# Issuing the expert-row gathers of a PEER layer in pairs of one table instead of in turn

## The chip, the cores and the metric

The kernel runs on one core of one Trainium2 chip. The metric is the device time of one execution in microseconds; the median of several runs counts. The engines are TensorE (PE in the profile), VectorE (DVE), ScalarE (ACT), GpSimd (POOL, here called Pool) and SyncE (SP). Indirect transfers, which fetch one table row per partition, are issued by Pool.

## What is computed

One decoder layer on 1024 tokens of width 1024, all in float32: attention and a convolution side by side, an output projection, and then the expert retrieval (PEER), in which nearly all the bytes are moved. Cut to its core:

```python
for each chunk of 128 tokens:
    s1, s2 = scores of the query halves against 128 + 128 keys, for 8 heads
    top_s, experts = best 16 of the 16 x 16 candidate sums          # 128 experts per token
    gates = softmax(top_s)
    act = gelu(einsum('chkd,cd->chk', u_tab[experts], xc))           # one u row per expert
    y = einsum('chk,chkd->cd', gates * act, v_tab[experts])          # one v row per expert
```

Each of the two tables has 16384 rows of 4 KB. Each token reads its own 128 rows from each of them.

## The kernel before, in words

There are two phases. Phase 0 projects all tokens and brings the first chunk up to its list of experts. Phase 1 runs over the 8 chunks; in step (c, f) it retrieves the rows of chunk c while it computes the attention, convolution, mixing, query and search of chunk f = c + 1 ("the front") in between. A step has 128 slots, one for each expert. The program is written out by hand for each engine, and each engine executes its list in order; semaphores connect them.

In slot s:

- Pool (`step` and `gather` at the gpsimd block) issues the gather of u row s of chunk c, and of v row s - 20 (LAG = 20; in the first 20 slots these are the last v rows of the chunk before). A gather brings 128 rows of 4 KB, one to each partition, 512 KB.
- VectorE (`dot_row`, L1744) multiplies the landed u row by the tokens' vector and sums; this increments `dotted` and frees the u slot. Then come the pieces of the front that VectorE has in this slot.
- ScalarE applies gelu to 16 dots at a time and builds for each expert a diagonal matrix of its weights (`spread_weight`, L1577).
- TensorE (`add_row`, L1433) multiplies the diagonal by the landed v row and adds it to the sum y in PSUM: two products of 512 columns, each shown in the records as two MATMULs, so four for one row; this increments `row_added` and frees the v slot. Then come TensorE's pieces of the front in that slot.
- In slot 20, `begin_y` (L1422) starts the sum of the new chunk, once ScalarE has copied the old one out (L1583).

Rows land in two rings of six slots, `ring_u` and `ring_v`. Before each gather Pool waits until the row that had the slot six rows earlier was used:

```python
if before >= 0 and kind == "u":
    hold(pool, dotted, before + 1, pool_passed)
...
elif before >= 0:
    hold(pool, row_added, pe_rows(before), pool_passed)
```

Since Pool works in order, a gather that has to wait holds back all gathers behind it. After the last chunk's slots, `tail` issues the last 20 v rows. VectorE adds five of the last 20 aside (`SIDE`), TensorE the others.

Of the kernel before, what the change touches and what calls it, by code (L numbers as in the profile page):

```python
# [37 lines left out]
ROWS = PH * TOPK  # L38
# [4 lines left out]
LAG = 20  # L43
SLOTS = ROWS
# [40 lines left out]
def row_of(c, e):  # L85

    return ROWS * c + e


def hold(eng, sem, value, passed):  # L90

    eng.wait_ge(sem, value)
    eng.sem_inc(passed, 1)


def later(i):

    return not isinstance(i, int) or i > 0
# [1111 lines left out]
def phase1(nc, S, base, psum, ident, ident_b, mask, kT, vals, keys_bd, w_kept, wo_sb, actT, qT,  # L1210
# [38 lines left out]
    def pe_rows(n):  # L1249

        return n + 1 - len([t for t in SIDE if row_of(CHUNKS - 1, t) <= n])
# [23 lines left out]
    def over_chunks(step):  # L1275

        step(None, 0)
        for f in range(1, CHUNKS):
            step(f - 1, f)
        step(CHUNKS - 1, None)  # L1280

    with nc.Block() as block:

        @block.sync
        def _(sp):
            def load_front(f):
                if later(f):
                    sp.wait_ge(S.z_ready, UNITS * f)
                    sp.dma_start(qT[:, :, :].rearrange("p b t -> p (b t)"),
                                 qT_spill[f]).then_inc(S.q_in, 16)  # L1290
                    sp.wait_ge(S.tapped, TAP_OPS * f)
                    sp.dma_start(conv_in[:, :, :], hT_spill[:, :, f * P:f * P + HALO + P]).then_inc(S.c_in, 16)
                    sp.wait_ge(y_begun, f)
                    sp.dma_start(S.h_res[:, :], x[0, f * P:(f + 1) * P, :]).then_inc(S.x_in, 16)

            def store(c):
                sp.wait_ge(y_copied, c + 1)
                sp.dma_start(out[0, c * P:(c + 1) * P, :], y_out[:, :]).then_inc(y_stored, 16)

            def step(c, f):  # L1300
                if f is not None:
                    load_front(f)
                if c is not None and later(c):
                    store(c - 1)

            over_chunks(step)
            store(CHUNKS - 1)
            sp.wait_ge(y_stored, 16 * CHUNKS)

        @block.gpsimd  # L1310
        def _(pool):
            def step(c, f):
                if c is None:
                    return
                hold(pool, S.experts_done, c + 1, pool_passed)
                for s in range(SLOTS):
                    gather("u", c, s)
                    if s >= LAG:
                        gather("v", c, s - LAG)
                    elif later(c):  # L1320
                        gather("v", c - 1, s - LAG + ROWS)

            def gather(kind, c, e):

                n = row_of(c, e)
                before = n - RING[kind]
                if before >= 0 and kind == "u":
                    hold(pool, dotted, before + 1, pool_passed)
                elif before >= 0 and in_side(before // ROWS, before % ROWS):
                    hold(pool, side_added, SIDE.index(before % ROWS) + 1, pool_passed)  # L1330
                elif before >= 0:
                    hold(pool, row_added, pe_rows(before), pool_passed)
                at = n % RING[kind]
                nc.gpsimd.indirect_dma_start(  # L1334
                    ring[kind][:, at, :], None, peer_u[0] if kind == "u" else peer_v[0],
                    bass.IndirectOffsetOnAxis(S.experts[c % 2][:, e:e + 1], 0)).then_inc(row_in[kind][at], 16)

            def tail():
                for e in range(ROWS - LAG, ROWS):
                    gather("v", CHUNKS - 1, e)  # L1340

            over_chunks(step)
            tail()

# [535 lines left out]
```

## Time and profile before

| | |
|---|---|
| median of 3 runs | 3085.05 us (3084.18 to 3085.98) |
| profiled execution | 3088.14 us, span 3086.4 us |
| TensorE / VectorE / ScalarE / Pool busy | 87% / 70% / 29% / 64% of the span |
| gathers | 2048, of 0.524 MB each |
| first gather, last gather issued | 365 us, 3074 us |
| data rate over the span | 363 GB/s |

A busy TensorE is not one at its peak, as the ends of its matmuls are modelled. In a timeline a line gives the start, the duration, the engine with the line of the source, what was done, and in brackets how long the engine sat idle before it and what ended that. Several instructions of one kind that follow on each other are merged, with their number. The name behind the arrow is inferred from semaphore events and can be that of another event close in time; for a wait on `row_added` or `dotted` the order of the program tells which it is.

### The profile page before, as it was taken

The numbers are of one execution on the slowest core, as the hardware profiler recorded it, in microseconds if no ns is written. First come the engines' busy times: TensorE is split into PE (matmuls) and PEld (weight loads), VectorE is DVE, ScalarE is ACT, GpSimd is POOL, SyncE is SP. The second block draws the span as 40 slices with busy tenths as digits, with TensorE's granted clock in tenths as the row PEclk, the third lists the DMA queues.
The fourth block names the chain that finished last, engine by engine and source line by source line (L and its number), as shares of the span: only waits on it lengthen the run. The fifth ranks groups of instructions, "written<-read, shape, count | busy, mean of one in ns | idle before, by whom it ended". The sixth has DMA issues, their size and how long they took to land.

```text
span 3086.4 us, 30095 instructions
## 1 busy us (share of the span) xinstructions
PE 2677.0 (87%) x7609; PEld 1207.5 (39%) x7609; DVE 2156.1 (70%) x5205; ACT 879.9 (29%) x2053; POOL 1986.3 (64%) x2062
## 2 busy tenths in 40 slices
PE   8999669878997889889997999799988999777777
PEld 4455324423352335334442445234433445222222
DVE  1161997886789667977788778977787767844443
ACT  2233123124221342135212542146213641111111
POOL 1000167777777777777777776776777677777775
PEclk9999879999999999999999999999999999999999
DMA  6011399999999999999999999999999999999998
GB/s 241 29 33 72 129 340 409 409 406 410 408 396 400 409 408 408 400 407 409 405 388 410 409 408 403 405 407 383 409 409 409 371 401 409 409 410 410 410 409 338
DMA packets 320463, 1121.47 MB, mean 363 GB/s; under 512 B 36465, under 2 KB 44681, under 8 KB 320296
## 3 DMA queue, kind: packets, MB, share of 16 engines
q0 software_dynamic: 294912, 1073.87, 88.0%
q1 hardware_dynamic: 25384, 45.72, 4.2%
q8 instruction: 62, 1.02, 0.1%
q14 instruction: 105, 0.86, 0.1%
HBM read 1111.01 MB, written 8.45 MB: 363 GB/s over the span
## 4 chain that ended last, share of the span: by engine, by line
PE 33%; DMA 24%; issue 12%; POOL 9%; DVE 8%; ACT 2%; POOLq 0%; ACTq 0%; DVEq 0%; SPq 0%
PE psum L1433 23%; DMA ring_v<-in_peer_v,experts 19%; POOL ring_v L1334 5%; DMA ring_u<-in_peer_u,experts 5%; POOL ring_u L1334 4%; PE psum L949 3%; DVE ring_u L1744 3%; PE psum L970 3%; PE psum L1365 1%; PE psum L1391 1%; ACT diag L1577 1%; PE psum L1381 1%; DVE acc L1700 1%; DVE top_i L1081 1%; DVE relu_z L1084 1%
## 5 line engine op out<-in xcount | busy, mean ns | idle before, releaser
L1433 PE MATMUL psum<-ring_v,diag 128*128 128x512 f32 x4076 | 1949.8, 604 | 331.3 <-DMA ring_v<-in_peer_v,experts 200.3
L1744 DVE CUSTOM_DVE_ANT_0 ring_u<-ring_u,psum 128x1024 f32<-128x1024 f32 x1024 | 1240.9, 1217 | 545.9 <-DMA ring_u<-in_peer_u,experts 540.3
L1334 POOL DMA_INDIRECT ring_u<-in_peer_u,experts x1024 | 983.7, 961 | 692.4 <-issue 594.2
L1334 POOL DMA_INDIRECT ring_v<-in_peer_v,experts x1024 | 991.8, 969 | 395.9 <-issue 243.4
L1433 PEld LDWEIGHTS psum<-ring_v,diag 128*128 128x128 f32 x4076 | 710.5, 190 | 1336.6 <-issue 961.3
L1577 ACT ACTIVATE diag<-ident,weights 128x128 f32<-128x128 f32 x1019 | 364.4, 393 | 771.1 <-PE psum L1433 550.6
L483 PE MATMUL psum<-w_sb,xnT 128*128 128x512 f32 x560 | 246.9, 599 | 0.3 <-DMA w_sb<-in_w_in 0.3
L1700 DVE SCALAR_TENSOR_TENSOR acc<-conv_in,taps,acc 128x128 f32<-128x128 f32 x840 | 239.6, 347 | 0.1
L483 PEld LDWEIGHTS psum<-w_sb,xnT 128*128 128x128 f32 x560 | 106.4, 193 | 128.1 <-issue 124.0
L970 PEld LDWEIGHTS psum<-actT,w_kept 128*128 128x128 f32 x1024 | 129.9, 192 | 47.4 <-issue 47.4
L1669 DVE TENSOR_TENSOR_SCAN log_keep<-log_keep,relu_z 128x256 f32<-128x256 f32 (+3 forms) x88 | 90.3, 1027 | 59.5 <-ACT log_keep L1510 58.1
L970 PE MATMUL psum<-actT,w_kept 128*128 128x128 f32 x1024 | 130.3, 275 | 0.0
L1525 ACT ACTIVATE attT<-psum 128x256 f32<-128x256 f32 (+3 forms) x88 | 44.9, 510 | 243.3 <-PE psum L1381 243.3
L949 PE MATMUL psum<-wo_sb,actT 128*128 128x512 f32 x224 | 112.1, 592 | 0.0
L1568 ACT ACTIVATE geld<-dots 128x16 f32<-128x16 f32 x64 | 13.8, 216 | 341.8 <-DVE dots L1744 341.5
L1365 PE MATMUL psum<-kT,qT 64*128 64x512 f32 (+3 forms) x176 | 86.6, 573 | 7.9 <-DMA qT<-qT_spill 6.9
L1744 DVE DVE_READ_ACCUMULATOR2_ANT dots<- 128x1 f32 x1024 | 85.0, 83 | 0.0
L1391 PEld LDWEIGHTS psum<-vals,attT 128*128 128x128 f32 x560 | 72.9, 195 | 29.2 <-issue 25.9
L1516 ACT ACTIVATE relu_z<-relu_z 128x256 f32<-128x256 f32 (+3 forms) x88 | 47.2, 536 | 117.7 <-DVE relu_z L1671 117.7
L1381 PE MATMUL psum<-ident,relu_z 128*128 128x128 f32 x280 | 48.2, 285 | 33.3 <-ACT relu_z L1516 33.2
L1391 PE MATMUL psum<-vals,attT 128*128 128x64 f32 x560 | 71.3, 275 | 2.5 <-ACT attT L1525 2.3
L790 DVE TENSOR_REDUCE qk_stat<-squares 128x16 f32<-128x1024 f32 x8 | 9.8, 1220 | 85.1 <-ACT squares L640 85.1
(188 smaller groups left out, 1556.3 us busy)
## 6 DMA issues: line engine op xcount, KB each, us to landing
ring_u<-in_peer_u,experts POOLq DMA_INDIRECT x1024, 10.0
ring_v<-in_peer_v,experts POOLq DMA_INDIRECT x1024, 9.9
w_sb<-in_w_in SPq DMA_DIRECT2D x4, 2048.0 KB, 19.6
x_in<-in_x SPq DMA_DIRECT2D x8, 512.0 KB, 4.0
w_kept<-in_w_out SPq DMA_DIRECT2D x1, 4096.0 KB, 13.6
h_res<-in_x SPq DMA_DIRECT2D x8, 512.0 KB, 6.7
w_kept<-in_peer_wq SPq DMA_DIRECT2D x1, 4096.0 KB, 14.5
wo_sb<-in_w_out SPq DMA_DIRECT2D x1, 4096.0 KB, 12.5
```

The costliest lines, as they stand in the source:

```text
L483: last = nc.tensor.matmul(ps[g], xT(i)[:, k, :], w_sb[:, g, k, :], start=k == 0, stop=k == KT_D - 1)
L949: product = nc.tensor.matmul(z[0][:, j * BANK:(j + 1) * BANK], S.actT[:, k, :], wo_sb[:, k, j * BANK:(j + 1) * BANK], start=k == 0, stop=k ...
L970: product = nc.tensor.matmul(z[0][:, h * P:(h + 1) * P], wq_sb[:, k, h * P:(h + 1) * P], S.actT[:, k, :], start=k == 0, stop=k == KT_D - 1)
L1334: nc.gpsimd.indirect_dma_start(ring[kind][:, at, :], None, peer_u[0] if kind == "u" else peer_v[0], bass.IndirectOffsetOnAxis(S.experts[c ...
L1365: last = nc.tensor.matmul(z, qT[lo:lo + HD, a // 2, :], kT[lo:lo + HD, a // 2, lo_key:hi_key], start=True, stop=not has_own)
L1381: last = nc.tensor.transpose(t_ps[:, s - lo:s - lo + P], S.relu_z[a % 2][:, s:s + P], ident[:, :])
L1391: last = nc.tensor.matmul(o_ps[:, a * HD:(a + 1) * HD], S.attT[:, b, :], vals[:, b, a * HD:(a + 1) * HD], start=n == 0, stop=n == len(orde ...
L1433: last = nc.tensor.matmul(y_ps[:, j * BANK:(j + 1) * BANK], diag[:, e % DIAGS, :], ring["v"][:, n % RING["v"], j * BANK:(j + 1) * BANK], s ...
L1577: nc.scalar.activation(diag[:, e % DIAGS, :], ident[:, :], ACT.Copy, scale=weights[:, e:e + 1]).then_inc(diagonal, 1)
L1669: nc.vector.tensor_tensor_scan(l[:, back], l[:, back], r[:, back], carry, ALU.add, ALU.add).then_inc(S.summed, counts(f))
L1700: nc.vector.scalar_tensor_tensor(out=acc[:, c, :], in0=conv_in[:, c, t:t + P], scalar=taps[:, c, t:t + 1], in1=acc[:, c, :], op0=ALU.mult, ...
L1744: nc.vector.tensor_tensor_reduce(out=row, in0=row, in1=hn, scale=1.0, scalar=0.0, op0=ALU.mult, op1=ALU.add, accum_out=dots[:, e:e + 1]).t ...
```

## The change

Pool's loop goes over two slots at a time. It issues the two u gathers of the two slots and then their two v gathers. Which slot, semaphore and value each gather waits for, and which list of experts it reads, are as before; the other engines' programs are the same.

```diff
                 hold(pool, S.experts_done, c + 1, pool_passed)
-                for s in range(SLOTS):
+                for s in range(0, SLOTS, 2):
                     gather("u", c, s)
-                    if s >= LAG:
-                        gather("v", c, s - LAG)
-                    elif later(c):
-                        gather("v", c - 1, s - LAG + ROWS)
+                    gather("u", c, s + 1)
+                    for n in (s, s + 1):
+                        if n >= LAG:
+                            gather("v", c, n - LAG)
+                        elif later(c):
+                            gather("v", c - 1, n - LAG + ROWS)
```

First Pool's queue where phase 1 begins. `experts0` is the list of experts of the even chunks; "x5" says that a row stands five times in a row. Before:

```order
L1334 DMA ring_u_1823<-in_peer_u,experts0_73 128x1024 [waits experts_done]
L1334 DMA ring_u_1823<-in_peer_u,experts0_73 128x1024 x5
L1334 DMA ring_u_1823<-in_peer_u,experts0_73 128x1024 [waits dotted] x15
L1334 DMA ring_v_1824<-in_peer_v,experts0_73 128x1024
L1334 DMA ring_u_1823<-in_peer_u,experts0_73 128x1024 [waits dotted]
L1334 DMA ring_v_1824<-in_peer_v,experts0_73 128x1024
```

The same place in the changed kernel:

```order
L1336 DMA ring_u_1823<-in_peer_u,experts0_73 128x1024 [waits experts_done]
L1336 DMA ring_u_1823<-in_peer_u,experts0_73 128x1024 x5
L1336 DMA ring_u_1823<-in_peer_u,experts0_73 128x1024 [waits dotted] x16
L1336 DMA ring_v_1824<-in_peer_v,experts0_73 128x1024 x2
L1336 DMA ring_u_1823<-in_peer_u,experts0_73 128x1024 [waits dotted] x2
```

22 u gathers stand ahead of the first v gather instead of 21, and from there on they go two by two.

Then Pool's queue where the second chunk begins (`experts1` is its list, `experts0` still that of the first chunk's last v rows). Before:

```order
L1334 DMA ring_v_1824<-in_peer_v,experts0_73 128x1024 [waits row_added]
L1334 DMA ring_u_1823<-in_peer_u,experts1_74 128x1024 [waits experts_done,dotted]
L1334 DMA ring_v_1824<-in_peer_v,experts0_73 128x1024 [waits row_added]
L1334 DMA ring_u_1823<-in_peer_u,experts1_74 128x1024 [waits dotted]
L1334 DMA ring_v_1824<-in_peer_v,experts0_73 128x1024 [waits row_added]
```

And in the changed kernel:

```order
L1336 DMA ring_v_1824<-in_peer_v,experts0_73 128x1024 [waits row_added] x2
L1336 DMA ring_u_1823<-in_peer_u,experts1_74 128x1024 [waits experts_done,dotted]
L1336 DMA ring_u_1823<-in_peer_u,experts1_74 128x1024 [waits dotted]
L1336 DMA ring_v_1824<-in_peer_v,experts0_73 128x1024 [waits row_added] x2
L1336 DMA ring_u_1823<-in_peer_u,experts1_74 128x1024 [waits dotted] x2
```

The second u gather of a pair has moved ahead of the first v gather, with its wait for `dotted`; the waits themselves are the same. An even chunk length and an even LAG keep the pairs aligned with the slots throughout.

## Rows read from the trace of the kernel before

**Rows 1.** The page: busy time by engine, and the data rate in 40 slices.

```profile
PE 2677.0 (87%) x7609; PEld 1207.5 (39%) x7609; DVE 2156.1 (70%) x5205; ACT 879.9 (29%) x2053; POOL 1986.3 (64%) x2062
...
GB/s 241 29 33 72 129 340 409 409 406 410 408 396 400 409 408 408 400 407 409 405 388 410 409 408 403 405 407 383 409 409 409 371 401 409 409 410 410 410 409 338
```

**Rows 2.** The page's DMA queues: packets, MB, share of 16 engines.

```profile
q0 software_dynamic: 294912, 1073.87, 88.0%
```

**Rows 3.** Windows: length, busy PE, PEld, DVE, ACT, POOL; PEclk, DMA share, GB/s.

```profile
410.00:3040.00 2630.00, 2283.83 (x6430) 1010.74 (x6430) 1960.93 (x4636) 760.71 (x1810) 1935.68 (x2008) 1.00 1.02 404
400.00:450.00 50.00, 31.98 (x81) 14.20 (x82) 46.75 (x119) 18.62 (x46) 34.97 (x38) 0.80 0.95 356
900.00:950.00 50.00, 42.59 (x117) 18.94 (x117) 48.94 (x188) 7.05 (x20) 35.96 (x37) 1.00 0.99 376
2100.00:2150.00 50.00, 47.98 (x172) 24.84 (x172) 35.97 (x68) 28.04 (x61) 32.57 (x35) 0.97 0.98 371
2440.00:2450.00 10.00, 8.58 (x16) 3.86 (x17) 3.52 (x7) 2.99 (x6) 3.70 (x4) 0.66 0.97 345
2450.00:2500.00 50.00, 49.32 (x188) 26.19 (x187) 39.48 (x72) 31.79 (x67) 37.78 (x37) 1.00 0.97 365
2700.00:2750.00 50.00, 38.54 (x80) 13.48 (x80) 25.02 (x41) 7.29 (x20) 37.66 (x41) 1.00 1.03 409
```

**Rows 4.** Groups of lines, Pool, 410 to 3040 us: busy, mean ns, idle before.

```profile
L1334 POOL DMA_INDIRECT ring_v<-in_peer_v,experts x1004 | 972.2, 968 | 379.5 <-issue 240.7 <-DVE dots L1744 75.2 <-PE psum L1433 63.6
L1334 POOL DMA_INDIRECT ring_u<-in_peer_u,experts x1004 | 964.0, 960 | 314.5 <-issue 238.2 <-PE psum L1433 49.1 <-DVE dots L1744 27.2
```

**Rows 5.** Timeline of all engines near 1510 us, while the front mixes.

```profile
1508.67 1.88 PE L1433 MATMUL psum<-ring_v,diag 128*128 128x512 f32 x4
...
1510.38 1.02 PE L949 MATMUL psum<-wo_sb,actT 128*128 128x512 f32 x2
...
1511.24 1.88 PE L1433 MATMUL psum<-ring_v,diag 128*128 128x512 f32 x4
1511.33 1.22 DVE L1744 CUSTOM_DVE_ANT_0 ring_u<-ring_u,psum 128x1024 f32<-128x1024 f32 x1 [1.29 <-DMA ring_u<-in_peer_u,experts]
...
1512.47 0.08 DVE L1744 DVE_READ_ACCUMULATOR2_ANT dots<- 128x1 f32 x1
...
1512.60 1.03 POOL L1334 DMA_INDIRECT ring_u<-in_peer_u,experts  x1 [0.30 <-issue]
...
1513.94 0.93 POOL L1334 DMA_INDIRECT ring_v<-in_peer_v,experts  x1 [0.30 <-issue]
```

**Rows 6.** ring_v, issue to landing: issued 1500 to 1520, then 940 to 950.

```profile
DMA to landing us min/median/max: 11.4/11.5/12.4
...
DMA to landing us min/median/max: 7.2/7.3/7.4
```

**Rows 7.** Waits of TensorE, 420 to 3040 us: total, times, longest.

```profile
PE psum L1433 <- DMA ring_v<-in_peer_v,experts: 195.3, 304, 1.6
```

**Rows 8.** Timeline where the chunk's sum begins, all engines.

```profile
2440.26 1.02 ACT L1583 ACTIVATE hn_next<-psum 128x1024 f32<-128x1024 f32 x1
...
2441.42 3.75 PE L1422 MATMUL psum<-h_res,ident 128*128 128x512 f32 x4 [1.75 <-ACT hn_next L1583]
...
2442.45 0.93 POOL L1334 DMA_INDIRECT ring_u<-in_peer_u,experts  x1 [0.30 <-DVE dots L1744]
...
2444.97 3.14 PE L1433 MATMUL psum<-ring_v,diag 128*128 128x512 f32 x4
...
2448.91 0.93 POOL L1334 DMA_INDIRECT ring_v<-in_peer_v,experts  x1 [5.54 <-PE psum L1433]
...
2450.15 0.93 POOL L1334 DMA_INDIRECT ring_u<-in_peer_u,experts  x1 [0.30 <-issue]
...
2451.36 1.28 DVE L1669 TENSOR_TENSOR_SCAN log_keep<-log_keep,relu_z 128x512 f32<-128x512 f32 x1 [7.85 <-ACT log_keep L1510]
```

**Rows 9.** Timeline of TensorE in a stretch with rows only.

```profile
2720.44 1.96 PE L1433 MATMUL psum<-ring_v,diag 128*128 128x512 f32 x4 [0.61 <-DMA ring_v<-in_peer_v,experts]
```

## The prediction

> **What bounds the kernel now.** I read the page's slices first. From the seventh slice on the GB/s row stands near 409, slice after slice, while no engine is that steadily full [rows 1]. The software queue moved 1073.87 MB, which is 2048 gathers of 0.524 MB [rows 2]; at 409 GB/s one gather takes 0.524/409 = 1.28 us, a u and v pair 2.56 us. The steady part is therefore paced by the transfers.
>
> Then the question is how often the transfers are not fed. Over 410 to 3040 us the mean is 404 GB/s against 409.5 when full [rows 3], so (409.5 - 404)/409.5 x 2630 = 35 us are lost there; 6.5 us of these ((409.5 - 356)/409.5 x 50) belong to the start between 400 and 450 us, where only u rows come. The remaining 29 us sit in a few dips: 900 to 950 us (376 GB/s, 4.1 us), 2100 to 2150 (371, 4.7 us), 2440 to 2450 (345, 1.6 us), 2450 to 2500 (365, 5.4 us) [rows 3], and smaller ones. Of the page's slices 7 to 39, eight stand below 405 (396, 400, 400, 388, 403, 383, 371, 401) [rows 1]. A new order of the same 2048 gathers can win at most these 29 us; the floor of 1.28 us each stays.
>
> Third, who holds Pool. Its gathers cost 960 ns (u) and 968 ns (v), and the smallest gap before one is 0.30 us (the u gather in [rows 5]). 1004 such gaps are 301 us. Before the u gathers the idle time is 314.5 us, 13 us more than that; before the v gathers it is 379.5 us, 78 us more [rows 4]. So Pool waits nearly always for a v slot, which TensorE frees, and hardly ever for a u slot, which VectorE frees. Pool has 0.94 + 0.30 = 1.24 us per gather against the transfers' 1.28: once its queue is drained it gains only 0.04 us per gather.
>
> **How full the queue is.** Where it is full, the cycle of a v slot shows why. At 1511.24 us a row starts on TensorE, ends 1.88 us later at 1513.12, and the v gather that waited for it starts at 1513.94, 0.82 us after [rows 5]. Issue to landing is 11.5 us there [rows 6]. 11.5 + 1.88 + 0.82 = 14.2 of the 12 x 1.28 = 15.4 us between two uses of a slot; 1.2 us go into the wait before the row. Around 940 us issue to landing is 7.3 us [rows 6] and the dip of 900 to 950 us is open: I take 7.3 as an estimate of the drained end. The cushion is 11.5 - 7.3 = about 4 us.
>
> **The change, part by part.** No gather, wait or byte is added or removed on any engine. In each group of four, the first u and the last v keep their places. The odd u comes one place (1.28 us) earlier; the even v comes one place later. A slot's previous user is still 12 places ahead, since rings of 6 are three pairs.
>
> *Pool's own time*: same 1.24 us per gather, four in 4.96 us against 5.12 us of transfer. Zero, covered by the transfers; without that cover it would be zero too, the count being the same.
>
> *The odd u, earlier*: VectorE needs 1.22 + 0.08 = 1.30 us per dot [rows 5], so two that land 1.28 us apart are taken in turn. Work between them delays the odd dot and holds the odd u's successor, and the two v gathers queued behind it on Pool. The u slots had 13 us of waiting in the whole run against 78 for v [rows 4], so I take zero; the bound above is in the slower rival.
>
> *The even v, later*: here is a cost. TensorE is in order. Where it has mixing work between rows (two matmuls, 0.86 us from 1510.38 to 1511.24, after 1.71 us of row from 1508.67), rows come 2.57 us apart [rows 5]. Two v rows landing 1.28 us apart leave the second waiting 2.57 - 1.28 = 1.29 us longer than an evenly spaced one. Its slot frees later, so the full queue is 11.5 - 1.3 = 10.2 us deep. In a stretch with rows only, the row takes 1.72 us, and the loss is 1.72 - 1.28 = 0.44 us. While the cushion holds this costs nothing. A dip that begins with a full cushion then loses up to 1.29 us more; one that begins with the queue already drained loses nothing more, since Pool runs free. If TensorE is behind anyway, rows wait for it and not for landings, and the price is zero. Of the waits of rows, 304 (195.3 us) end on a landed v row [rows 7], of about 1000, so TensorE is often not behind. I count four dips of the first kind (the search stages of four chunks, of which 900 us is one) at the middle of 0 and 1.29: 4 x 0.65 = +2.6 us; bounds 0 and +5.2.
>
> *The odd u ahead of a blocked v*: here is a gain. At the chunk's 20th slot TensorE waits for the copy of the finished sum, then starts a new one. At 2442.45 us Pool issues a u and is then held 5.54 us, until 2448.91, for the first row of the new chunk; that held gather is v 6, an even one. The next u starts at 2450.15, after the minimal 0.30 us, and VectorE had finished no dot since about 2443.5 (it sat idle for 7.85 us before 2451.36) [rows 8]. Its slot was thus free all along. In the new order this u is issued before the hold, one transfer, 1.28 us, more for the queue in a place where the rate fell to 345 [rows 3]. Two chunks (2100, 2440) have such a dip: bounds 0 and -2.56, I take half, -1.3 us. The other half is given back because VectorE, stalled on the attention chain, holds the following odd u.
>
> *Start and end*: the first v goes out one u later (1.24 us), inside the start that VectorE limits; at the end the last v has its old place, and the chain of odd rows that leads to it too. I take +0.6, bounds 0 and +1.28.
>
> Sum: 2.6 - 1.3 + 0.6 = +1.9 us. The profiled execution took 3088.14 us (its span is 3086.4), so it would take 3090.0; the median of the runs, 3.1 us below the profiled one, moves from 3085.05 to **3087.0 us**. That is +0.06%: a measurement of this kernel can't tell anything within 0.2% (6.2 us) from no change.
>
> **Rivals.**
> *Cushion lost everywhere (slower).* The 1.29 us is lost at each of the eight slow slices [rows 1], and at the two deep dips twice, as the odd u's hold adds the same: 10 x 1.29 = +13 us, 3098. For it: Pool gains 0.04 us per gather, so a lost cushion of 1.29 us needs 32 gathers to return. Against it: at 7.3 us the queue was already drained in the middle of dips, and there order can't matter. It decides from five full losses on (6.4 us).
> *TensorE's clock (slower).* At 2441.42 TensorE starts after 1.75 us idle; the granted clock over 2440 to 2450 us is 0.66, a mix of the levels 2.4 and 1.2 GHz, and a row takes 3.14 us against 1.88 [rows 3, 5, 8]. Now, with rows only, TensorE idles 0.61 us before each row [rows 9]; with pairs it would idle 5.12 - 1.72 - 1.96 = 1.44 us before every second one. If the clock falls there, a row takes 1.26 us more. This decides only once more than (2.56 - 1.88)/1.26 = 54% of rows are slow; before that rows still keep pace. Were 80% slow over the 133 pitches of 2700 to 3040 us, it would cost 133 x (0.8 x 3.14 + 0.2 x 1.88 - 2.56) = 44 us. The Trainium skill (TensorE: Matmul & The Clock Gate, Part 1: The HAM clock gate) says that idleness lowers TensorE's clock and sustained activity restores it; by that, slow rows that fill the gaps should bring the clock back. The trace agrees in that the next window has 1.00 [rows 3]. So I give it little.
> *Holds covered (faster).* If the earlier u covers v holds wherever the rate dips and TensorE is behind at all of them, the cost term is zero and each of the eight slices gains up to 1.28 us: -10 us, 3075. For it: v is what holds Pool. Against it: the odd v is not issued sooner, so at the end of each group of four nothing is ahead. It decides from five full gains on.
> *The order on chip does nothing*: covered by my forecast.
>
> **How the numbers follow.** Forecast (a sum within 6.2 us of zero) 0.52; cushion lost everywhere 0.25; clock 0.05; holds covered 0.18. So slower 0.30, same 0.52, faster 0.18. The likeliest alone is 3083 to 3091 us (its bounds: -2.6 to +6.5 us). For 8 in 10 I reach into both sides, to 3077 and 3099.
>
> **What would show it.** Right: the GB/s row stays at 409 between dips, the number of gathers and Pool's time per gather are unchanged, issue to landing near 1500 us drops from 11.5 to about 10.2 us, waits of TensorE on v rows become fewer and longer, the hold at the new chunk's first row shrinks by about 1.2 us, and 2450 to 2500 us moves little. Wrong: a deeper queue, Pool waiting for u slots (much more than 13 us), clock below 1.00 in the row-only stretches, or a steady rate other than 409, which would mean that the order of tables itself matters to the transfers; no row of before bears on that.

## The result: slower, by more than forecast

| | before | after |
|---|---|---|
| median of 6 runs each | 3084.61 us (3083.91 to 3087.91) | 3101.54 us (3096.12 to 3103.47) |
| ratio after/before | | 1.0049, 95% interval 1.0038 to 1.006 |
| profiled execution | 3088.14 us | 3096.74 us, span 3094.9 us |

The change costs 16.9 us at the median (15.3 us at the mean, from which the ratio is taken); +1.9 us were forecast. The two profiled executions lie 8.6 us apart: that of before is above its median, that of after near the lowest of its runs. What the two traces show can therefore account for 8.6 us, not for all 16.9.

The page of after, busy time and rate, answers to [rows 1]:

```profile
PE 2630.9 (85%) x7609; PEld 1233.1 (40%) x7609; DVE 2139.8 (69%) x5205; ACT 882.0 (28%) x2053; POOL 2010.3 (65%) x2062
...
GB/s 240 29 32 72 133 338 409 396 400 409 408 404 390 404 408 409 399 400 407 408 383 399 409 408 396 407 400 401 409 403 401 393 397 406 394 410 410 409 409 351
```

The steady rate is still 409, so the floor of 1.28 us for a gather stands. But Pool is busy 24 us longer with the same 2062 instructions (2010.3 against 1986.3), and there are more slices a little below 409. Windows of after, with the columns of [rows 3]:

```profile
410.00:3040.00 2630.00, 2233.05 (x6416) 1034.44 (x6417) 1940.15 (x4630) 761.59 (x1807) 1952.28 (x2001) 0.99 1.02 403
900.00:950.00 50.00, 41.64 (x117) 19.98 (x116) 49.05 (x189) 7.05 (x20) 35.27 (x36) 0.97 0.99 382
1000.00:1050.00 50.00, 38.40 (x94) 15.61 (x94) 32.02 (x55) 16.07 (x33) 38.18 (x39) 1.00 1.01 392
2100.00:2150.00 50.00, 47.99 (x169) 23.97 (x168) 34.40 (x61) 32.35 (x67) 35.72 (x36) 1.00 1.02 401
2440.00:2450.00 10.00, 9.15 (x30) 3.90 (x29) 7.37 (x14) 8.04 (x15) 6.37 (x7) 1.00 1.02 405
2450.00:2500.00 50.00, 48.06 (x181) 25.48 (x182) 36.54 (x66) 30.30 (x63) 35.09 (x36) 1.00 0.98 374
2700.00:2750.00 50.00, 36.36 (x77) 14.47 (x78) 25.68 (x45) 7.00 (x19) 37.81 (x41) 0.97 1.02 401
```

In this trace the windows at the new chunks gained (371 to 401, 345 to 405, 365 to 374 against [rows 3]): 3.7 + 1.5 + 1.1 = 6.3 us. The loss is elsewhere, in many small pieces such as 1000 to 1050 us (351 GB/s in its first 10 us), which ran at the full 409 before:

```profile
1000.00:1050.00 50.00, 41.30 (x99) 15.35 (x98) 34.97 (x60) 15.51 (x31) 38.10 (x40) 1.00 1.03 409
```

Summed over all 50-us windows from 450 to 3050 us, each missing rate taken as (409.5 - rate)/409.5 x 50, before lost 31.4 us and after 41.1. The difference of 9.7 us agrees with the 8.6 between the profiled executions.

Pool's two groups of after, 410 to 3040 us, answer to [rows 4]:

```profile
L1336 POOL DMA_INDIRECT ring_u<-in_peer_u,experts x1001 | 985.6, 985 | 346.3 <-issue 259.6 <-DVE dots L1746 51.9 <-PE psum L1435 34.9
L1336 POOL DMA_INDIRECT ring_v<-in_peer_v,experts x1000 | 966.8, 967 | 331.5 <-issue 256.1 <-PE psum L1435 42.7 <-DVE dots L1746 32.6
```

Less 0.30 us for each gather, the holds are 346.3 - 300.3 = 46 us before u and 31.5 us before v, together 77.5; before they were 13 + 78 = 91. So Pool waits 14 us less and works 24 us more. The u gather's mean went from 960 to 985 ns. The prediction watched the waits and took the work as fixed.

**Why a gather takes longer.** The timeline of after, Pool and VectorE, where VectorE looks up the chosen experts (L1163 compares with an index table, L1171 multiplies by the table entries):

```profile
1005.15 1.22 DVE L1171 TENSOR_TENSOR relu_z<-relu_z,attT 128x1024 f32<-128x1024 f32 x1
1005.22 1.96 POOL L1336 DMA_INDIRECT ring_v<-in_peer_v,experts  x1 [0.30 <-issue]
```

And the same operations in before:

```profile
1003.42 1.22 DVE L1171 TENSOR_TENSOR relu_z<-relu_z,attT 128x1024 f32<-128x1024 f32 x1
...
1004.44 1.02 POOL L1334 DMA_INDIRECT ring_v<-in_peer_v,experts  x1 [0.30 <-issue]
```

A gather that starts under this product ends 0.81 us after it: 1006.37 + 0.81 = 1007.18 in after, 1004.64 + 0.82 = 1005.46 in before. It pays nearly the whole overlap: 1.15 us of overlap cost 1.02 us in after, 0.20 us cost 0.08 in before. In before, VectorE and Pool both step by 2.56 us, and 26 of the 28 gathers that start under this product do so 0.9 to 1.15 us behind its start, near its end. With pairs, 13 of 28 start 0.06 to 0.09 us behind its start and pay nearly everything, and 12 start 0.58 to 0.74 us behind it and pay 0.35 to 0.5 us.

I tabulated each gather of 430 to 3035 us by what covered its start. The excess over 0.937 us sums to 54.4 us in before and 76.8 in after, 22 of the 24 us that Pool works more; under the product L1171 alone it went from 4.4 us to 19.5 us. All gathers that start more than 0.04 us into L1163 or L1171, with more than 0.16 us of it to come, are lengthened (49 of 49 in before, 47 of 47 in after). Of those that start so under the dot product (L1744 in before), which has one of its inputs in PSUM, none is (0 of 801, 0 of 754). Those that start just ahead of an instruction with two SBUF inputs keep 0.94. By the Trainium skill (SBUF — State Buffer, Who interferes with whom) an instruction of VectorE with two SBUF inputs contends with one of GpSimd that reads SBUF, the shared port pair is an exclusive lock, and the order of issue decides who blocks. The trace agrees, with these counts; what a gather of this program reads from SBUF is its list of experts. The same section infers that tensor_tensor does not delay descriptor generation; here gathers under it took up to 1.96 us for 0.94.

**How full the queue is.** ring_v of after, issue to landing, answers to [rows 6] (issued 1500 to 1520, then 940 to 950), and below it 1020 to 1040:

```profile
DMA to landing us min/median/max: 10.2/11.1/11.3
...
DMA to landing us min/median/max: 5.5/6.0/6.1
...
DMA to landing us min/median/max: 6.5/6.8/8.0
```

Before, 1020 to 1040 us had refilled to a median of 10.4; after, it is still at 6.8. In [rows 3]'s dip of 900 to 950 us the queue is drained, and afterwards Pool wins back only 0.04 us per gather. The queue is less deep in other places too. At 880 to 897 us, ahead of the dip, the median is 11.5 in before and 9.0 in after. Over the v gathers of the chunks 1 to 6, it falls from 11.5 to 10.3 in slots 50 to 57, where the queue is fullest, and from 8.9 to 6.7 in slots 96 to 103, from where the look-up follows.

TensorE's waits of after, 420 to 3040 us, answer to [rows 7]:

```profile
PE psum L1435 <- DMA ring_v<-in_peer_v,experts: 365.9, 277, 4.4
...
PE psum L1435 <- ACT diag L1579: 10.9, 9, 1.4
```

And the second of these lines in before:

```profile
PE psum L1433 <- ACT diag L1577: 129.7, 215, 1.2
```

Behind them TensorE in the rows-only stretch, answering to [rows 9]:

```profile
2717.42 3.67 PE L1435 MATMUL psum<-ring_v,diag 128*128 128x512 f32 x8 [1.44 <-DMA ring_v<-in_peer_v,experts]
2722.54 3.67 PE L1435 MATMUL psum<-ring_v,diag 128*128 128x512 f32 x8 [1.45 <-DMA ring_v<-in_peer_v,experts]
```

Waits for landed rows are fewer and longer. Part of their growth is exchange: 215 waits of before for ScalarE's diagonal have become 9. Both kinds together were 325 us in 519 waits and are now 377 us in 286. Rows come in pairs ("x8" is two rows) 5.12 us apart with a pause of 1.44 us, the predicted one.

And the start of a chunk, Pool, answering to [rows 8]:

```profile
2443.17 0.94 POOL L1336 DMA_INDIRECT ring_v<-in_peer_v,experts  x1 [0.30 <-issue]
...
2445.84 1.92 POOL L1336 DMA_INDIRECT ring_u<-in_peer_u,experts  x1 [0.49 <-issue]
2449.69 1.05 POOL L1336 DMA_INDIRECT ring_u<-in_peer_u,experts  x1 [1.92 <-DVE dots L1746]
```

The hold of 5.54 us is gone; the longest near it is 1.92 us, on a u slot. At the other deep dip, around 2103 us, before held Pool 4.00 us on a v slot, and after at most 0.68.

### The profile page after: what moved, and what is told of

It is laid out like the page before. It is cut to its first block, busy times and chain, and to the rows that moved or that the text cites. A ratio compares the mean times of both kernels' runs of the same rounds, so it can differ in the third digit from the quotient of the medians.

```text
span 3094.9 us, 30095 instructions
## 1 busy us (share of the span) xinstructions
PE 2630.9 (85%) x7609; PEld 1233.1 (40%) x7609; DVE 2139.8 (69%) x5205; ACT 882.0 (28%) x2053; POOL 2010.3 (65%) x2062
## 3 DMA queue, kind: packets, MB, share of 16 engines
q8 instruction: 62, 1.02, 0.1%
## 4 chain that ended last, share of the span: by engine, by line
PE 32%; DMA 24%; issue 12%; DVE 10%; POOL 8%; ACT 2%; POOLq 0%; ACTq 0%; DVEq 0%; SPq 0%
PE psum L1435 22%; DMA ring_v<-in_peer_v,experts 19%; DMA ring_u<-in_peer_u,experts 5%; POOL ring_u L1336 4%; DVE ring_u L1746 4%; POOL ring_v L1336 4%; PE psum L949 3%; PE psum L970 3%; PE psum L1367 1%; PE psum L1393 1%; PE psum L1383 1%; DVE top_i L1081 1%; DVE relu_z L1084 1%; DVE top_v L1077 1%; DVE acc L1702 1%
## 5 line engine op out<-in xcount | busy, mean ns | idle before, releaser
L1435 PE MATMUL psum<-ring_v,diag 128*128 128x512 f32 x4076 | 1906.9, 604 | 385.3 <-DMA ring_v<-in_peer_v,experts 373.9
L1336 POOL DMA_INDIRECT ring_u<-in_peer_u,experts x1024 | 1008.2, 985 | 724.5 <-issue 615.6
L1435 PEld LDWEIGHTS psum<-ring_v,diag 128*128 128x128 f32 x4076 | 736.5, 192 | 1320.4 <-issue 1044.5
L1383 PEld LDWEIGHTS psum<-ident,relu_z 128*128 128x128 f32 x280 | 33.9, 143 | 85.2 <-issue 44.6
## 6 DMA issues: line engine op xcount, KB each, us to landing
w_kept<-in_peer_wq SPq DMA_DIRECT2D x1, 4096.0 KB, 14.7
```

Of the source, the lines that this page charges most:

```text
L1336: nc.gpsimd.indirect_dma_start(ring[kind][:, at, :], None, peer_u[0] if kind == "u" else peer_v[0], bass.IndirectOffsetOnAxis(S.experts[c ...
L1383: last = nc.tensor.transpose(t_ps[:, s - lo:s - lo + P], S.relu_z[a % 2][:, s:s + P], ident[:, :])
L1435: last = nc.tensor.matmul(y_ps[:, j * BANK:(j + 1) * BANK], diag[:, e % DIAGS, :], ring["v"][:, n % RING["v"], j * BANK:(j + 1) * BANK], s ...
```

## The experiments

Four theories were set against each other. A: gathers lengthened under VectorE's look-up. B: the pairs make the queue shallower or its refill slower in general (the second v of a pair waits, the prediction's slower rival). C: TensorE's clock, as a consequence of the pauses. D: odd u gathers held behind VectorE's long search pieces. Where an expectation gives them other names or words, its own stand.

On some chips the transfers ran at about 355 instead of 409 GB/s, whatever the kernel, and the kernel before took 3429 to 3451 us there, so every run is compared only with the kernel before on its own chip.

### First set, 355 GB/s: by slots, and with the tables in PSUM

`pairs_last24` pairs only in slots 104 to 127, `pairs_first104` only in slots 0 to 103:

```diff
-                for s in range(SLOTS):
+                for s in range(0, SLOTS, 2):
                     gather("u", c, s)
...
+                    if s >= 104:      # pairs_first104: s < 104
+                        gather("u", c, s + 1)
+                        v(s)
+                    else:
+                        v(s)
+                        gather("u", c, s + 1)
+                    v(s + 1)
```

> Pairs only in Pool's slots 104 to 127 of each chunk, where VectorE does the twelve look-up pieces; u and v in turn in the other 104 slots. Before is 3084.6 us, all pairs 3101.5 (+16.9). Theory A (gathers are lengthened under VectorE instructions with two SBUF inputs, and the pairs move them under the look-up's products): most of the loss is made here, +8 to +15 us, and the look-up line's share of lengthened gathers rises as with all pairs. Theory B (a shallower queue at every dip, my slower rival): only a fifth of the slots are changed, +0 to +4 us.

> The complement: pairs in slots 0 to 103, u and v in turn in 104 to 127. Theory A: little is left of the loss, +2 to +8 us. Theory B: nearly all of it stays, +12 to +17 us.

`pairs_psum_tables` has all pairs, and the look-up reads its tables from a PSUM bank that is free at that time, so that its operations have only one SBUF input (L1163 and L1171 of after); `turn_psum_tables` has the same tables with the order of before:

```diff
-def vector_front(nc, dve, S, z):
+def vector_front(nc, dve, S, z, tables=None):
...
+    if tables is not None:
+        tf = tables[:, 0:2 * ROWS].rearrange("p (h two k) -> p h two k", two=2, k=TOPK)
+        parts = tables[:, 2 * ROWS:4 * ROWS]
...
-    = vector_front(nc, dve, S, (z_ps, w_ps))
+    = vector_front(nc, dve, S, (z_ps, w_ps), t_ps)
```

> All pairs; in phase 1 the look-up's two tables (top indices as floats, split positions) stand in PSUM, so that the look-up's comparisons and products have one SBUF input and not two. Same elements, counts and waits. Theory A: no gather is lengthened under those two lines (24.3 us of Pool's time in the pairs kernel), and 10 to 16 of the 16.9 us come back: 3086 to 3091. Theory B: the queue's depth is set by the order alone, 3099 to 3102.

> The order of before with the same tables in PSUM. Lengthened gathers under the look-up's two lines are 11 us in before. Theory A: Pool gains these 11 us, of which a part shows, since the queue is drained at some of these places only: 0 to 6 us faster, 3079 to 3085. Theory B: no change.

| | median | before, same chip | ratio (95%) |
|---|---|---|---|
| pairs_last24 | 3455.77 | 3450.94 | 1.0016 (1.0005 to 1.0028) |
| pairs_first104 | 3454.25 | 3450.94 | 1.0018 (1.0003 to 1.0033) |
| pairs_psum_tables | 3454.46 | 3450.94 | 1.0008 (0.999 to 1.0026) |
| turn_psum_tables | 3444.87 | 3450.94 | 0.999 (0.9975 to 1.0006) |

Inconclusive: the intervals are as wide as the effect, and the full change had no run of its own on that chip.

### Second set, again 355 GB/s, with the full change beside them

> The changed kernel itself once more, beside the others of this call. The call before ran where the transfers reached only about 355 GB/s (before took 3450.9 us there), so its small differences say little about a kernel that is bound at 409. At 409 GB/s: +0.4 to +0.6% against before, both theories. At 355 GB/s Pool has 1.48 - 1.24 = 0.24 us to spare per gather and not 0.04, the queue refills six times as fast: 0 to +0.3%.

> All pairs with the look-up's tables in PSUM, again, for the case that this call's transfers run at 409 GB/s. Theory A (gathers lengthened under VectorE's instructions with two SBUF inputs): 10 to 16 us faster than all pairs, within 0.2% of before. Theory B (queue depth from the order alone): as all pairs, +0.4 to +0.5% against before.

> u and v in turn with the tables in PSUM, again. Theory A: 0 to 6 us faster than before at 409 GB/s. Theory B: no change.

> Pairs only in slots 104 to 127 (24 of 128), again. Theory A: +8 to +15 us against before at 409 GB/s. Theory B: +0 to +4 us.

| | median | before, same chip | ratio (95%) |
|---|---|---|---|
| pairs_all | 3454.16 | 3446.17 | 1.0027 (1.001 to 1.0045) |
| pairs_psum_again | 3451.55 | 3446.17 | 1.0014 (0.9999 to 1.0029) |
| turn_psum_again | 3442.06 | 3446.17 | 0.9981 (0.9967 to 0.9995) |
| pairs_last24_again | 3445.48 | 3446.17 | 0.9991 (0.9977 to 1.0005) |

At 355 GB/s a gather's transfer takes 0.524/355 = 1.48 us, and Pool's 1.24 leave it 0.24 us of room instead of 0.04. The full change costs 8.0 us there (ratio 1.0027) instead of 16.9. Pool is as slow as on the other chips (2012.6 us busy in `pairs_all`, 1970.7 in `pairs_psum_again`). That the loss shrinks where Pool has more room agrees with A and B; the intervals, 1.001 to 1.0045 and 1.0038 to 1.006, overlap slightly, so it isn't shown. One result doesn't fit A's interplay: at 355 GB/s the tables in PSUM gained as much with the order of before (4.1 us here, 6.1 in the first set) as with pairs (2.6 us here), all near the width of the intervals.

### Third set: shorter gathers, to restore the ratio

On such a chip I tried to bring the transfer back to 1.28 us by gathering 896 of 1024 columns of each row. These four kernels leave out an eighth of each table row and read other places of the tables, so their output is another one.

```diff
-                    ring[kind][:, at, :], None, peer_u[0] if kind == "u" else peer_v[0],
+                    ring[kind][:, at, 0:896], None, bass.AP(table.tensor, table.offset, [[896, 16384], [1, 896]]),
```

> The two calls before met transfers at about 355 GB/s, 1.48 us per gather, where Pool (1.24 us) has room. This kernel brings that ratio back to where it was: each gather moves 896 and not 1024 floats per row (taken from other places of the tables, the last 128 columns are zero, so the output isn't the reference's; dots and products still run over 1024). 0.459 MB at 355 GB/s is 1.29 us. u and v in turn: the control. Expected about 3110 us there, if the transfers set the pace. On a chip at 409 GB/s a gather would take 1.12 us and Pool's 1.24 would be the bound.

> The same with all pairs. Both theories: +0.4 to +0.6% against the short gathers in turn, if at 1.29 us per gather the loss is that of 409 GB/s. If Pool is the bound (409 GB/s), theory A gives the whole lengthening of gathers, +18 us, theory B less.

> Short gathers, all pairs, look-up's tables in PSUM. Theory A (gathers lengthened under VectorE's instructions with two SBUF inputs): at least 10 us below short pairs, and within 0.2% of short in turn. Theory B (queue depth by the order alone): as short pairs.

> Short gathers in turn, tables in PSUM: closes the square. Theory A: 0 to 6 us below short in turn, so the gap between the two orders shrinks from about 15 to under 8 us. Theory B: the gap of the two orders is the same with either place of the tables.

Against 3429.4 us of the unshortened kernel before on that chip: `short_turn` 3416.55 us (0.9976), `short_pairs` 3421.08 (0.9982), `short_pairs_psum` 3419.25 (0.9976), `short_turn_psum` 3413.16 (0.9966). 12.5% fewer bytes save 0.4% of the time in `short_turn`; its rate over 410 to 3040 us falls from about 355 to 314 GB/s. So a gather is no shorter than before on this chip, and the attempt missed its condition. The pairs are slower with either place of the tables, by 4.5 us and, with the tables in PSUM, 6.1 us; A expected the second difference to be the smaller one. Both are smaller than the intervals.

### Fourth set, 409 GB/s: the clock, and the tables again

`pairs_warm` fills TensorE's pauses: all pairs, and behind every second row, in the rows-only parts, four products with a zero tile that add nothing to the sum:

```diff
+                if e % 2 and not is_last and (c == CHUNKS - 1 or 73 <= e < 101):
+                    for _ in range(4):
+                        nc.tensor.matmul(y_ps[:, 0:BANK], ident_b[:, :], nothing[:, :], start=False, stop=False)
```

> All pairs, and behind every second row, in the look-up's slots and in all of the last chunk, four bf16 products of a zero tile added to the sum (about 0.86 us of TensorE, the result is unchanged), so that TensorE's pause before a pair shrinks from 1.4 to about 0.6 us. Theory C (my clock rival: the pairs' pauses lower TensorE's clock, late rows hold v slots): falls of the clock in those stretches vanish and 8 to 16 us of the 16.9 come back. Theories A and B: the falls go, the time stays within 4 us of all pairs.

Measured: 3104.13 us against 3084.56, ratio 1.0063 (1.005 to 1.0077). TensorE was busy 2764.8 us instead of 2630.9, and its waits for v rows fell from 365.9 to 244.3 us, so the pauses were filled. But the clock fell as often after 430 us (11 times; 11 in after, 3 in before), so the condition of the test, that the falls vanish, wasn't met, and that no time came back doesn't decide. Against C speaks the next kernel: its trace has 12 such falls, and it is 8.7 us faster at the median than the full change. And `pairs_psum_turn58to110`, below, has 5 and still costs 6.7 us. So C isn't what these 8.7 us were, and little speaks for it in the rest; what the falls cost isn't shown.

> All pairs with the look-up's tables in PSUM, for a chip with transfers at 409 GB/s (before near 3085 us). Theory A: 3086 to 3091 us. Theory B: 3099 to 3102. At 355 GB/s again: +0.1% against before, as twice.

Measured on the same chip: 3092.81 us against 3084.56, ratio 1.0027 (1.0017 to 1.0036). The interval lies below that of the full change (1.0038 to 1.006), and 8.7 of the 16.9 us are gone (6.6 of 15.3 at the means). The full change itself has no run on this chip; `pairs_warm`, which has all pairs and its tables in SBUF, has, and is 11.3 us slower. The median lies between the expected ranges of A and B. The place seen above, in this kernel:

```profile
1004.73 1.22 DVE L1174 TENSOR_TENSOR relu_z<-relu_z,psum 128x1024 f32<-128x1024 f32 x1
...
1005.20 0.94 POOL L1339 DMA_INDIRECT ring_v<-in_peer_v,experts  x1 [0.30 <-issue]
```

The gather starts inside the product, and takes 0.94 us, since the product now has one input in PSUM. And the rate:

```profile
1000.00:1050.00 50.00, 39.94 (x98) 16.17 (x96) 33.60 (x55) 16.91 (x35) 37.72 (x39) 1.00 1.03 409
```

The window is full again (after: 392), and issue to landing over 1020 to 1040 us is back at a median of 10.2 us. Pool is busy 1976.9 us, less than before. No gather is lengthened any more under the two instructions (0 of 48). A stands, for about half of the loss. One reservation: the profiled execution of this kernel was its slowest run (3097.25 us), so the comparison of two profiled executions doesn't show the 8.7 us; the medians do, and the stretch does.

### Fifth set, 409 GB/s: the parts

> u and v in turn with the look-up's tables in PSUM, for a chip at 409 GB/s. Theory A: since the gathers in turn are lengthened by only 11 us under those lines and the queue refills there, 0 to 5 us faster than before.

> Pairs only in slots 104 to 127 (mostly the look-up), tables in SBUF. All pairs lose 16.9 us at 409 GB/s, 8.7 of them come back with the tables in PSUM. Theory A with D: +6 to +10 us. Theory B: +1 to +4.

> Pairs only in slots 0 to 103, tables in SBUF. Theory A with D: the other part, +6 to +10 us. Theory B: +13 to +16.

`pairs_psum_turn58to110` has the tables in PSUM and pairs everywhere but in slots 58 to 109, where the search and the look-up run (`not 58 <= s < 110` in place of `s >= 104`, with the diff of the tables):

> Tables in PSUM, and the pairs everywhere but in Pool's slots 58 to 109 of each chunk, where u and v go in turn: there VectorE has its long pieces (residual, search), and in the traces of the pairs the odd u waits up to 2.3 us for its dot behind them. Theory D (that wait is the rest of the loss, about 8 us at 409 GB/s beside the port's 9): within 3 us of the kernel with tables in PSUM and all in turn. Theory B (depth lost to pairs anywhere, most in the mixing slots before 58): at least 5 us above it, as all pairs with tables in PSUM (3092.8).

| against 3085.38 us of before | median | ratio (95%) | Pool busy | lost rate |
|---|---|---|---|---|
| turn_psum_third | 3085.11 | 1.0 (0.9991 to 1.0009) | 1973.1 | 32.1 us |
| pairs_last24_third | 3087.75 | 1.0011 (1.0002 to 1.002) | 2004.1 | 30.4 us |
| pairs_first104_third | 3091.93 | 1.0024 (1.0014 to 1.0034) | 1992.8 | 34.4 us |
| pairs_psum_turn58to110 | 3092.07 | 1.0024 (1.0015 to 1.0034) | 1973.4 | 33.8 us |
| fourth set: pairs_psum_third | 3092.81 | 1.0027 (1.0017 to 1.0036) | 1976.9 | 38.7 us |
| after | 3101.54 | 1.0049 (1.0038 to 1.006) | 2010.3 | 41.1 us |

"Lost rate" is the sum over the windows, as above, of one profiled execution each. The last two rows were measured on other chips, against 3084.56 and 3084.61 us.

The traces also tell where the rate is lost, if each stretch runs from the issue of the u gather of one slot to that of another, over all chunks (us of missing rate against 409.5; one trace each, so differences of a few us mean little):

| | slots 20 to 43 | slots 80 to 103 | slots 104 to 127 | median issue to landing of v, slots 96 to 103 |
|---|---|---|---|---|
| before | 16.9 | 11.5 | 1.6 | 8.9 us |
| turn_psum_third | 15.9 | 12.1 | 0.4 | 8.9 |
| pairs_last24_third | 13.4 | 6.4 | 8.3 | 9.2 |
| pairs_first104_third | 14.4 | 14.9 | 0.3 | 6.8 |
| pairs_psum_turn58to110 | 19.1 | 7.4 | 0.3 | 8.9 |
| pairs_psum_third | 19.8 | 18.3 | 0.3 | 6.7 |
| pairs_warm | 16.4 | 15.8 | 14.6 | 6.7 |
| after | 12.2 | 17.8 | 13.1 | 6.7 |

In the look-up's slots, more than 1.6 us is lost only where pairs and tables in SBUF meet.

- With the order of before, tables in PSUM save Pool 13 us and the run nothing. Its holds grow in return (390.2 + 318.6 us idle against 379.5 + 314.5). Lengthened gathers are covered there, as the prediction assumed; with the pairs they are not. So it is an interaction of the two. (A expected 0 to 5 us faster.)
- Pairs in slots 104 to 127 alone lengthen nearly as many gathers under the look-up (18.7 us under L1171, after 19.5) and cost only 2.4 us, where A had expected 6 to 10 and B 1 to 4. Pairs in the other slots alone cost 6.5 us (A expected 6 to 10, B 13 to 16). Together they cost 16.9, not 8.9 (15.3 against 9.4 at the means, on another chip). The look-up lies where the queue refills after the search's dip. The table fits this reading: with pairs in the last slots alone the queue comes into the look-up 9.2 us deep, and slots 80 to 127 lose 14.7 us, hardly more than the 13.1 of before; with pairs everywhere it comes 6.7 us deep, and they lose 30.9. The longer gathers cost little in the first case and much in the second.
- In-turn order in slots 58 to 109 brings 8.2 to 6.7 us against before, about 1.5 us, less than the intervals. D, which expected at most 3 us above `turn_psum_third` and got 7.0, falls as it stands, for the search's slots. The hold that it speaks of is real: at 906.85 us, at the end of a chunk's search, a u gather of after waited 2.32 us for a dot, where one of before had waited 0.96 us. `pairs_psum_third` has it too (2.33).

6.7 us remain that neither the look-up nor the search slots explain. They belong to pairs in slots 0 to 57 and 110 to 127. The queue is a little shallower there (slots 40 to 49: 11.4 us in `turn_psum_third`, 10.8 in `pairs_psum_turn58to110`, 10.4 in `pairs_psum_third`), as B says, but two waits could make it so: the even v's, which the prediction priced, and the odd u's outside the search. Holds of odd u gathers beyond 0.30 us sum to 8.6 us in before, 42.2 in after and still 38.2 in `pairs_psum_turn58to110`. No run takes the two apart, so which wait carries the rest stays open.

## Why the prediction was wrong

It forecast no measurable change (3087.0 us, 3077 to 3099); the kernel became 16.9 us slower, 3101.54 us, 2.5 us outside the range.

- **"Pool's own time: ... Zero, covered by the transfers; without that cover it would be zero too, the count being the same."** This step failed, and it is about half of the loss. The count is the same and the duration isn't: the order moves gathers under VectorE's look-up, and Pool works 24 us more. Without the part under the look-up 8.7 us are gone (1.0049 to 1.0027). The clue stood in [rows 4] and [rows 5]: means of 960 and 968 ns, where single gathers took 0.93 us and one took 1.03. I used these as a fixed cost and never asked what the long ones had in common.
- **"The even v, later": "the full queue is 11.5 - 1.3 = 10.2 us deep", 4 dips x 0.65 = +2.6 us.** The depth of the full queue came out near it: 10.3 us in slots 50 to 57, though 11.1 at 1500 us and 12.0 against 12.2 at 2900 to 3000 us. What failed is "one that begins with the queue already drained loses nothing more, since Pool runs free": the drained queue is shallower too (940 to 950 us: 7.3 to 6.0), and its refill is slower (1020 to 1040 us: 10.4 to 6.8). The loss without the look-up's part, 8.2 us, is above the bound of 5.2. One reading behind the depth was wrong as well: the v gather at 1513.94 us did not wait 0.82 us for the row that ended at 1513.12, it followed the gather of 1512.60 us after the minimal 0.30 us. The sum doesn't use it.
- **"The odd u ahead of a blocked v": -1.3 us.** Right mechanism: the hold of 5.54 us shrank to at most 1.92, more than the 1.2 I named. The windows there gained 6.3 us in the trace of after, where I had the gain capped at one transfer for each dip. How large it is stays open, as the slots 20 to 43 lose 19.8 us in the trace of `pairs_psum_third`, more than the 16.9 of before.
- **"The odd u, earlier", "I take zero", for 13 us of waiting for u slots.** Too low: u holds are 46 us, which my list of what would show me wrong named. v holds fell by 47. The test of D puts the price in the search's slots at some 1.5 us; outside them it is open, and can be part of the 6.7 us.
- **Start and end, +0.6 us.** 400 to 450 us fell from 356 to 349 GB/s, 0.9 us; inside its bounds.
- **The rivals.** "Cushion lost everywhere" came nearest (3098, 0.25): losses at many places of about a transfer each, and the slow return by 0.04 us per gather. Its reason, 1.29 us at every dip, isn't what the runs showed for half of it, so that its number fits is in part luck. TensorE's clock: the pauses came as worked out (1.44 us), the falls too (3 to 11, with a granted clock of 0.97 over 2700 to 2750 us), but no run shows time in them. "Holds covered" was right at chunk starts alone.
- Right too: steady rate 409, number of gathers, TensorE's waits fewer (304 to 277) and longer (1.6 to 4.4 us at most). The forecast's sign, slower, was right, but by a sum in which half of the cause was missing.

## What to carry to other kernels

Before calling an instruction's cost unchanged by a new order, look at the spread of its durations and at what runs on the other engines under the long ones; a fixed phase between two engines may be what keeps the mean low. A queue whose feeder is only 3% faster than its drain (1.24 against 1.28 us) turns small losses into lasting ones: price a loss by whether the queue is full or refilling when it comes, and don't count on parts of a change to add (2.4 and 6.5 us apart, 16.9 together). A saving on such a feeder was worth nothing alone at 409 GB/s (tables in PSUM: 1.0) and 8.7 us beside the change that exposes it.

## What the runs showed of the hardware

- An indirect gather on Pool that starts under VectorE's comparison or product of the look-up, which have two SBUF inputs, ends 0.81 us after that instruction (0.94 us becomes up to 1.97; 96 of 96 well-covered gathers in the traces of before and after); with one of the inputs in PSUM it stays 0.94 (0 of 48 in `pairs_psum_third`).
- The same kernel had 409 GB/s on some chips and about 355 on others, 3085 against 3429 to 3451 us. The Trainium skill (DMA: Bandwidth & Descriptors, Measured) gives about 358 GB/s to a core whose neighbour streams as well; no run here shows what the neighbour did.
- At the lower rate, rows of 3.5 KB instead of 4 KB took about as long (3416.55 against 3429.4 us, at 314 GB/s), read from other places of the tables.
- The time doesn't follow the number of falls of TensorE's clock: 11 in after (3101.54 us) and 12 in `pairs_psum_third` (3092.81 us), against 3 in before. Filling the pauses of 1.44 us (TensorE busy 2764.8 us instead of 2630.9) left 11.
